# A two-layer encoder trunk: the second mixer's input projection with seven half-size products for each pair of column blocks

## The reference, cut to what matters

```python
def odd_mixer(xn, w_in, gate_bias, h_gain, w_out):
    u = xn @ w_in                      # xn (256, 1024), w_in (1024, 3104)
    q, k, v, o, gates = split(u, [512, 1024, 2048, 3072])
    ...
    h = rms_norm(h, h_gain) * sigmoid(o)
    return h @ w_out                   # (1024, 1024)
```

## Time and profile before

| | us |
|---|---|
| median of 3 runs | 1161.56 |
| lowest, highest | 1160.43, 1163.86 |
| the profiled execution's own time | 1162.22 |
| its span | 1160.4 |
| TensorE busy / VectorE busy / GpSimd busy | 879.7 / 237.3 / 41.5 |

### The profile page before, as it was taken

The page is one execution under the profiler, slowest core; times in us unless marked ns, Lnnn a source line. Parts: engine busy times, 40 slices in busy tenths (PEclk is TensorE's granted clock), DMA queues, the critical chain, the costliest instruction groups (busy, mean ns, idle before and its releaser), DMA issues.

```text
span 1160.4 us, 20228 instructions
## 1 busy us (share of the span) xinstructions
PE 879.7 (76%) x9135; PEld 510.6 (44%) x9135; DVE 237.3 (20%) x784; ACT 169.1 (15%) x459; POOL 41.5 (4%) x46
## 2 busy tenths in 40 slices
PE   9999995666576757566899999987575676666666
PEld 4454663434344434343544556644242443433343
DVE  2351421111012111110234435211110111111111
ACT  1141310101011101000224232211010110101011
POOL 1651000000000000000000000000000000000000
PEclk9999998879888887888999998988787787878789
DMA  9992999999999999999973258999999999999996
GB/s 347 336 324 99 380 428 425 429 425 429 426 428 426 426 429 424 429 426 425 393 292 118 100 227 353 383 424 429 426 428 426 426 428 425 430 425 427 426 426 271
DMA packets 46261, 439.26 MB, mean 379 GB/s; under 512 B 4640, under 2 KB 5888, under 8 KB 21344
## 3 DMA queue, kind: packets, MB, share of 16 engines
q1 hardware_dynamic: 43632, 433.96, 89.7%
q0 software_dynamic: 1088, 2.97, 1.1%
q10 hardware_dynamic: 1456, 1.04, 0.3%
HBM read 436.91 MB, written 1.05 MB: 377 GB/s over the span
## 4 chain that ended last, share of the span: by engine, by line
PE 48%; DMA 45%; another core or an unknown queue 2%; DVE 2%; ACT 1%; issue 1%; SPq 0%; POOL 0%; DVEq 0%
DMA mem<-in_moe_w_up 44%; PE psum L1311 43%; PE psum L1449 3%; PE psum L1441 1%; PE psum L1332 1%; DMA mem<-in_ev_w_in 1%; SPq L440 0%; DVE mem L962 0%; PE psum L1318 0%; ACT mem L645 0%; DVE mem L1112 0%; DVE mem L1108 0%; PE psum L1610 0%; PE psum L1376 0%
## 5 line engine op out<-in xcount | busy, mean ns | idle before, releaser
L1311 PE MATMUL psum<-mem 128*32 128x256 f32 (+3 forms) x7114 | 671.7, 438 | 258.8 <-DMA mem<-in_moe_w_up 226.2
L1311 PEld LDWEIGHTS psum<-mem 128*32 128x32 f32 (+2 forms) x7114 | 346.8, 132 | 554.9 <-issue 459.9
L1011 DVE TENSOR_TENSOR mem<-psum,mem 128x128 f32<-128x128 f32 x62 | 18.1, 291 | 645.6 <-ACT mem L659 645.6
L659 ACT ACTIVATE mem<-psum 128x128 f32<-128x128 f32 x62 | 17.2, 277 | 522.2 <-PE psum L1311 522.2
L1311 PE MATMUL psum<-mem,x 128*128 128x128 f32 (+1 forms) x576 | 71.5, 285 | 7.2 <-DVE mem L962 3.7
L1449 PE MATMUL psum<-mem 32*128 32x256 f32 x1024 | 73.3, 400 | 3.0 <-ACT mem L665 2.0
L1311 PEld LDWEIGHTS psum<-mem,x 128*128 128x128 f32 x576 | 69.5, 201 | 10.4 <-DVE mem L962 4.5
L1449 PEld LDWEIGHTS psum<-mem 32*128 32x128 f32 x1024 | 46.2, 184 | 30.7 <-issue 23.5
L970 DVE TENSOR_SCALAR mem<-cst,mem 128x128 f32<-128x128 f32 x124 | 37.2, 342 | 20.7 <-PE psum L1441 20.6
L665 ACT COPY mem<-psum 128x256 f32<-128x256 f32 x62 | 23.1, 372 | 95.2 <-PE psum L1311 95.2
L661 ACT COPY mem<-psum 128x256 f32<-128x256 f32 x62 | 23.1, 372 | 64.0 <-PE psum L1441 63.9
(11 more groups left out here) (168 smaller groups left out, 313.8 us busy)
## 6 DMA issues: line engine op xcount, KB each, us to landing
mem<-in_moe_w_gate SPq DMA_DIRECT2D x64, 2048.0 KB, 47.3
mem<-in_moe_w_up SPq DMA_DIRECT2D x64, 2048.0 KB, 48.0
mem<-in_moe_w_down SPq DMA_DIRECT2D x62, 2048.0 KB, 42.8
mem<-in_od_w_in SPq DMA_DIRECT2D x6, 2048.0 KB, 22.5
mem<-in_ev_w_in SPq DMA_DIRECT2D x3, 2048.0 KB, 19.4
mem<-in_ev_w_out SPq DMA_DIRECT2D x2, 2048.0 KB, 28.6
mem<-in_moe_w_down SPq DMA_DIRECT2D x4, 1024.0 KB, 41.9
mem<-in_od_w_out SPq DMA_DIRECT2D x2, 2048.0 KB, 20.0
```

The lines of the kernel that those rows point to most:

```text
L659: nc.scalar.activation(M["sg"], bank(4)[:, 0:P], ACT.Silu).then_inc(s["silu"], 1)
L1011: link(V.tensor_tensor(M["h"], src, M["sg"], ALU.mult))
L1311: return nc.tensor.matmul(out_, lhsT, rhs, start=start, stop=stop)
```

## The change

Blocks are taken in pairs (q,k), (o,o), (v,v). A pair is a product of a (2x2 of 128 tokens x 512) by a (2x2 of 512 x 512) matrix, and is done with seven products of quarter size in Winograd's form of Strassen's method: each is 4 matmuls of 512 columns where the eight of the plain form would be. The input needs four sums of 128x512 (`token_sum`, once), each pair four sums of weights of 128x2048 (two on VectorE, two on GpSimd), and the output sums are made as the banks are evicted. The o columns get their sigmoid afterwards, from SBUF.

```diff
-        ORDER_C = (0, 1, 4, 5, 2, 3)
-        BANK_C = (4, 2, 4, 6, 4, 6)
-        DENSE = {..., "C": (8, 9, 10, 0, 1, 2, 7, 8)}
-        RING = {..., "D": (0, 4, 1, 2, 3, 9, 6, 10, 5, 7, 8)}
+        PRODUCTS = ((1, 2, 5, 6, 3, 7, 4), (1, 5, 2, 6, 3, 7, 4), (1, 6, 2, 7, 4, 5, 3))
+        DENSE = {..., "C": (8, 9, 10, 0, 1, 2, 7, 0)}
+        RING = {..., "D": (4, 8, 1, 2, 3, 9, 6, 10, 5, 7, 0)}
 SyncE: the second half of w_out (j == 7) and the first pieces of D
-                    sp.wait_ge(used["C"], 1)
+                    sp.wait_ge(s_qTp["C"], 4)
+                    sp.wait_ge(s_dl, HEADS)
+                    expert_piece("D", 1, 0)
+                    sp.wait_ge(used["C"], product(2, 4))
                 sp.dma_start(dense_slot("C", j)..., dense_source("C", j))
...
+                if n == 1:
+                    sp.wait_ge(used["C"], product(2, 5))
+                elif n == 2:
+                    sp.wait_ge(used["C"], product(2, 4))
+                elif n == 3:
+                    sp.wait_ge(used["C"], product(2, 3))
 GpSimd
+            def block_sum_3(pair):
+                pool.wait_ge(s_tv, 2 * pair + 1)
+                pool.tensor_tensor(b12, b22, b12, ALU.subtract).then_inc(s_tp, 1)
+            def block_sum_4(pair):
+                pool.wait_ge(s_tv, 2 * pair + 2)
+                pool.wait_ge(used["C"], product(pair, 6))
+                pool.tensor_tensor(T2_at[pair], block_half(2 * pair, 1), T2_at[pair], ALU.subtract).then_inc(s_tp, 1)
+            def right_low(pair):
+                pool.wait_ge(s_ca, act_copy(pair, "m5"))
+                pool.wait_ge(s_cv, dve_sum(pair, "u3"))
+                pool.tensor_tensor(pair_out(pair, 1, 1), m5, m1_at[1], ALU.add).then_inc(s_cp, 1)
+            block_sum_3(0); block_sum_4(0); block_sum_3(1); right_low(0); block_sum_4(1)
+            block_sum_3(2); right_low(1); block_sum_4(2); right_low(2)
 ScalarE (copy_first evicts product 1 twice, once for each token half's scale)
-            copy_u(0)
+            copy_first(0)
+            left_high(0)
...
+            copy_first(2)
+            act.wait_ge(s_cv, dve_sum(1, "c21"))
+            act.wait_ge(s_cp, 2)
+            for t in range(TT):
+                nc.scalar.activation(og[:, t], og[:, t], ACT.Sigmoid).then_inc(s_og, 1)
+            left_high(2)
 VectorE
+            dve.wait_ge(s_xTv, 2 * DC + DC // 2)
+            token_sum(1, A21, A22, ALU.add, 0)
+            token_sum(2, S1, A11, ALU.subtract, 1)
             V.reduce_sum(C["fold"], ...)
-            copy_u(0)
+            block_sum_1(0)        # waits for blocks 0 and 1 to land
+            block_sum_2(0)        # waits for block_sum_1
             dve.wait_ge(s_gp, 1)
             V.tensor_copy(C["parts"], mbank(7)[:, 0:T]).then_inc(s_gpc, 1)
...
-            copy_u(1)
+            token_sum(4, ...); token_sum(3, ...); block_sum_1(1); add_sixth(0)
...
+            right_high(0); add_seventh(0); block_sum_2(1); left_low(0)
...
-            for h in range(HEADS):
+            for h in range(4):
                 decay(h)
+            block_sum_1(2); add_sixth(1); right_high(1); block_sum_2(2); decay(4)
+            add_seventh(1); decay(5); dve.wait_ge(s_tp, 4); decay(6); left_low(1); decay(7); add_sixth(2)
             (copies of the transposed q and k)
-            copy_u(4)
-            for h in range(4):
-                weigh(h)
+            weigh(0); weigh(1); add_seventh(2); weigh(2); weigh(3); left_low(2)
...
                 if h == 2:
-                    copy_u(5)
+                    right_high(2)
 TensorE
-            dense_block("C", 0, xnT_of(2), 0, DC + DC // 2)
+            first(0)
             (gate columns)
-            dense_block("C", 1, xnT_of(2), 6, midway=add_gate_parts)
+            second(0)             # waits for both copies of product 1
+            add_gate_parts()
+            fifth(0)
+            sixth(0)
             (transposes of the gates)
-            dense_block("C", 2, xnT_of(2), 0)
+            third(0); seventh(0); fourth(0); first(1)
             (transposes of the decays)
+            pe.wait_ge(s_cv, 4)
             m_on_all(0)
-            part(3, 2, 0, range(DC))
+            fifth(1); second(1); sixth(1); third(1)
             m_on_all(1)
-            part(3, 2, 1, range(DC)).then_inc(used["C"], 1)
+            seventh(1); fourth(1); first(2); sixth(2)
             (transposes of q and k)
-            dense_block("C", 4, xnT_of(2), 0)
+            second(2)
             ml_scores(0)
+            seventh(2)
             ml_scores(1)
-            part(5, 2, 0, range(0, 4))
+            fourth(2)
             numerators(0)         # now also waits for left_low(2) and left_high(2)
-            part(5, 2, 0, range(4, DC))
+            fifth(2)
             numerators(1)
             ml_scores(2)
-            part(5, 2, 1, range(0, 4))
+            third(2, range(0, 2))
             numerators(2)
             ml_scores(3)
-            part(5, 2, 1, range(4, DC)).then_inc(used["C"], 1)
+            third(2, range(2, 4))
             numerators(3)
```

More of the change, by code:

```diff
@@ new lines, in block_sum_2, with add_sixth @@
+            def block_sum_2(pair):
+                if pair == 1:
+                    dve.wait_ge(used["C"], product(0, 2))
+                    dve.wait_ge(s_tp, 2)
+                elif pair == 2:
+                    dve.wait_ge(used["C"], product(1, 3))
+                    dve.wait_ge(s_tp, 3)
+                dve.wait_ge(s_tv, 2 * pair + 1)
+                V.tensor_tensor(T2_at[pair], block_half(2 * pair + 1, 1), T1_at[pair], ALU.subtract).then_inc(s_tv, 1)
+            def add_sixth(pair):
+                dve.wait_ge(used["C"], product(pair, 6))
+                dve.wait_ge(s_ca, act_copy(pair, "m1"))
+                for t in range(TT):
+                    ins = V.scalar_tensor_tensor(m1_at[t], bank(BANKS[pair][6]), inv_rms(t), m1_at[t], ALU.mult, ALU.add)
+                ins.then_inc(s_cv, 1)
@@ L1225, in _ @@
             V.tensor_tensor(F_c, nM, F_c, ALU.subtract).then_inc(s_em, 1)
+            right_high(0)
+            add_seventh(0)
+            block_sum_2(1)
+            left_low(0)
             dve.wait_ge(s_aTp, 1)
@@ L1277, in h_normed @@
                                            og[:, t, o], ALU.mult, ALU.mult).then_inc(s_hn, 1)
-            for h in range(HEADS):
+            for h in range(4):
                 decay(h)
-            dve.wait_ge(s_og, 4)
+            block_sum_1(2)
+            add_sixth(1)
+            right_high(1)
+            block_sum_2(2)
+            decay(4)
+            add_seventh(1)
+            decay(5)
+            dve.wait_ge(s_tp, 4)
+            decay(6)
+            left_low(1)
+            decay(7)
+            add_sixth(2)
             for p in range(4):
@@ L1671, in _, with times @@
             wg = w_gates[:, :].rearrange("p (c n) -> p c n", c=DC)
-            dense_block("C", 0, xnT_of(2), 0, DC + DC // 2)
+            def times(pair, m, chunks=range(4)):
+                left, right = dense_slot("C", 2 * pair), dense_slot("C", 2 * pair + 1)
+                xn = xnT_of(2)
+                token, rows = {1: (xn[:, 0:4, 0:P], left[:, 0:2048]), 2: (xn[:, 4:8, 0:P], left[:, 2048:4096]),
+                               3: (S_at[4].rearrange("p (c t) -> p c t", c=4), right[:, 2048:4096]),
+                               4: (xn[:, 4:8, P:T], T2_at[pair]), 5: (S_at[1].rearrange("p (c t) -> p c t", c=4), T1_at[pair]),
+                               6: (S_at[2].rearrange("p (c t) -> p c t", c=4), T2_at[pair]),
+                               7: (S_at[3].rearrange("p (c t) -> p c t", c=4), right[:, 0:2048])}[m]
+                for c in chunks:
+                    if pair == 0 and m < 3:
+                        pe.wait_ge(s_xTv, DC + DC // 2 + 4 * (m - 1) + c + 1)
+                    last = nc.tensor.matmul(bank(BANKS[pair][m]), token[:, c], rows[:, c * 512:(c + 1) * 512],
+                                            start=c == 0 and m not in (2, 3), stop=c == 3, skip_group_check=m in (2, 3))
+                if chunks[-1] == 3:
+                    last.then_inc(used["C"], 1)
@@ new lines, in first, with second, third @@
+            def first(pair):
+                pe.wait_ge(*arrived["C", 2 * pair])
+                if pair == 1:
+                    pe.wait_ge(s_ca, act_copy(0, "c11"))
+                elif pair == 2:
+                    pe.wait_ge(s_cv, dve_sum(1, "c12"))
+                times(pair, 1)
+            def second(pair):
+                pe.wait_ge(s_ca, act_copy(pair, "m1"))
+                times(pair, 2)
+            def third(pair, chunks=range(4)):
+                pe.wait_ge(*arrived["C", 2 * pair + 1])
+                pe.wait_ge(s_sum, 3)
+                pe.wait_ge(s_ca, act_copy(pair, "m5"))
+                times(pair, 3, chunks)
@@ new lines, in sixth, with seventh @@
+            def sixth(pair):
+                pe.wait_ge(s_sum, 2)
+                pe.wait_ge(s_tv, 2 * pair + 2)
+                if pair == 1:
```

(18 more changed lines are left out.)

213 lines of the change are left out of this document (148 added, 65 removed).

## The result

| | us | runs |
|---|---|---|
| before, median (lowest to highest) | 1161.14 (1160.42 to 1163.86) | 5 |
| after, median (lowest to highest) | 1167.05 (1165.37 to 1169.35) | 5 |
| ratio, 95% interval | 1.0049 [1.0031, 1.0068] | |
| profiled execution after, its span | 1168.09, 1166.3 | 1 |

The change makes the kernel 5.9 us slower where 4.6 us faster was forecast, and the time lies above the range. What was forecast of the amount of work is there, what was forecast of the waits isn't.

A forecast was written before the change was run, and what follows sets the result against it. The end was taken to follow piece 11's issue, and that TensorE. Removed products -6.9 and waits +3.6 gave -3.3 us; with -1.3 behind, -4.6: 1161.9 to 1157.3 us, range 1154.9 to 1164.5.

The forecast's parts named there:

- Piece 11: Ring transfer of expert weights issued at 726.95 us when the first expert's product frees a slot; the end follows one for one.
- What is removed: TensorE's products fall from 96 to 84: 10.4 us in all, 6.9 of it up to the end of numerators(1).
- (a): TensorE's wait at second(0) for two ScalarE copies of product 1: 0.4 us.
- (b): TensorE's wait at add_gate_parts for VectorE's copy of the gate parts, behind two weight sums needing block 1: 2.3 us.
- (c): TensorE's wait at numerators(0) for left_low(2), right behind fourth(2): 0.9 us.
- What I cost at nothing: Other VectorE sums, GpSimd's six weight sums, ScalarE's sigmoids and SyncE's queue, all taken as covered, at no cost.
- Rival 2: GpSimd's block_sum_3(0), released with VectorE's block_sum_2(0), goes first and delays VectorE; slower by 1.1 to 5.5 us; chance 0.17.
- GpSimd's lengths: GpSimd's six weight sums of 2048 columns, taken at 4.5 us each from a two-input row of 2.18 ns a column.
- The prices at 4 and 5 ns a column: Cost if GpSimd's weight sums ran slower than taken: 0.8 us at 4 ns a column, 9.8 at 5.
- The tail: From head 1's divisors to project(0), VectorE is the chain: 14.0 instead of 15.16 us, -1.3; nothing changes from project(0) on.
- the stream hides nothing: Judges the rival that the weight stream, not piece 11's slot, sets the end, so time stays 1161.9 us; chance 0.05.
- rival 1: The new 2.3 us wait at add_gate_parts lowers TensorE's clock, costing 1.8 us: gain 2.8, time 1159.1 us; chance 0.19.

The follow-up runs named there:

- the kernel with the sums apart: Changed kernel, pair 0's GpSimd sums on VectorE, GpSimd's others started behind VectorE's second sum of the pair, gate parts copied earlier and added mid-product 2: 1155.96 us, ratio 0.9933.
- the fastest kernel: The kernel with the sums apart, plus the second head's scores, VectorE's left_low(2) and its weighings reordered ahead of the output projection: 1152.72 us, ratio 0.9903.
- the run with fills: Changed kernel with each of GpSimd's six block sums replaced by a fill of 2048 columns that reads nothing: 1159.53 us, ratio 0.9969.
- the run with 8 columns: Changed kernel with GpSimd's six block sums cut to 8 of their 2048 columns: 1159.86 us, ratio 0.9979.
- the kernel before with GpSimd reading: Kernel before, eight products, plus eight unused GpSimd subtractions of 1520 columns with both inputs in SBUF: 1172.83 us, ratio 1.0077.
- filler: Changed kernel with five unused matmuls of 512 columns put into TensorE's two waits around 603 to 606 us: 1165.22 us, ratio 1.0031.

## Why the prediction was wrong, by its own steps

- **What bounds the kernel**: right. Piece 11 decides, in eleven executions.
- **What is removed**, -6.9 us up to `numerators(1)` and 10.4 in all: right. In the kernel with the sums apart, head 1's divisors start at 651.60 against 655.94: -4.3, which is -6.9 with the waits 0.42 and 0.94 and a start of the products that was 0.8 us later, to within 0.4. The 10.4 in all isn't shown by itself: the fastest kernel gains 10.0 us, with the tail reordered and waits left.
- **The waits (a), (b), (c)**: 0.42, 1.42, 0.94 against 0.4, 2.3, 0.9. (b) is shorter because product 2 started and ended later; block 1 was seen at 573.6 and the sums took 2.29 us each, as taken. In other runs (b) was 1.37 to 2.90.
- **"What I cost at nothing"** is where it failed. VectorE's queue was followed with lengths measured where GpSimd was idle, and gave `left_low(0)` at 598 to 599; it was 605.57, some 7 us later. For a queue that isn't held up the forecast was right: with fills in the place of GpSimd's sums it is 598.53. The three stretched pieces are 8.9 us, more than the gap, because part of that time the queue would have spent waiting anyway (0.57 us for weights in the run with fills, 2.46 for the sixth product in that with 8 columns). `m_on_all(0)` waited 2.80 us, the transposes ahead of it 2.10, and the half clock behind them cost 3.3: 8.2 us, with no price in the sum. At head 1's divisors the kernel was 661.51 - 655.94 = 5.6 us later, where 3.3 earlier was forecast; of the 8.9 between, 8.2 less 0.9 (the shorter (b)) plus 0.8 (the later start) are placed, and 0.8 is not.
- **Rival 2** had the right mechanism and the wrong place. I asked only who wins where both sums are released together; VectorE does (575.98 against 576.03), as argued, and the forecast calls GpSimd's delay covered. It is, for GpSimd's result. But the delayed sum runs until 582.63 and then stands in front of the next VectorE instruction with both inputs in SBUF, 16 columns of the gate chain. A 4.5 us instruction on GpSimd collides with every such instruction in its 4.5 us, whoever released it, and the three that I hadn't looked at are not ties at all: GpSimd had begun 0.2 to 3.7 us earlier. Its price, 1.1 to 5.5 us slower, was near the 5.9 measured, but by another sum: that is luck.
- **GpSimd's lengths**: 4.52 us for 2048 columns, the 4.5 taken. No TensorE wait is released by GpSimd. The prices at 4 and 5 ns a column (0.8 and 9.8 us) stand there without a working, and no run came near them.
- **The tail**, -1.3 us: from head 1's divisors to `project(0)` it was 675.01 - 661.51 = 13.50 against 15.16, -1.7. "From `project(0)` on nothing changes" failed by 2.2 us in this execution. `project(0)` took 8.06 us, 1.4 more than in the earlier trace rows, as the half clock lasted longer; then the first expert's first products took 5.35 against 3.84, at a granted clock of 0.72 in 720 to 730 against 1.00, and the router's 3.73 against 4.50. That the change causes this isn't shown: behind the same waits (1.66 and 2.24) `project(0)` took 6.71 us in the run with 8 columns, and in the kernel before with GpSimd reading 8.05, behind a wait of 2.71 as against 2.70.
- **The other rivals**: the stream hides nothing. The clock (rival 1) fell, but at a wait of 4.9 us that wasn't there in the forecast; at (b) it fell only where (b) was 2.7 us and more (filler, 8 columns), not at 1.4.

## What to carry to other kernels

Work given to an idle GpSimd isn't free of VectorE: before a sum goes there, list the VectorE instructions in its whole duration that have two SBUF inputs, or go from SBUF to SBUF with one, however small, and add the rest of the GpSimd instruction to the first of them; a GpSimd instruction that follows at once can hold up another. Put GpSimd's SBUF work beside VectorE's PSUM reads, by a wait on VectorE's last SBUF sum. And compare an instruction's duration with that of its twin in the same trace: a hold-up of this kind shows there, and in no wait.

## What the runs showed of the hardware that was not expected

- VectorE's hold-up by GpSimd also meets instructions with one input that go from SBUF to SBUF: a `tensor_scalar` of 16 columns 3.44 us instead of 0.17, two copies of 128 columns 3.64 instead of 0.36. With one input in SBUF and the other in PSUM none was met (the decays, 1.39 us for four beside a GpSimd sum).
- It is symmetric: a GpSimd sum of 8 columns (0.20 us alone) took 2.29 us beside VectorE's sum in the run with 8 columns, and of 2048 columns 6.60 instead of 4.52.
- 29 us of GpSimd work for which nothing waits until some 90 us later made the kernel before 10.1 us slower.
- The clock's price behind a wait of 2.9 us was 2.6 us, nearly the wait again (9.69 against 7.11 us for the same products); behind one of 2.7 us, in the run with the filler, it was 1.3 (8.43).
